# Starting the first expert inside the router stage, turning the weight ring by four slots, and adding the second biases in the last sums

## The reference, cut to what matters

```python
h = layer_norm(DN_ALPHA * h + mixed, ln1_g, ln1_b)
# router: logits, top 4 of 32, softmax over the four
hb = x2[tok] @ w_exp_in[e] + b_exp_in[e]          # 1024 -> 2048
act = min(x_glu, 7) * sigmoid(1.702 * min(x_glu, 7)) * (clip(x_lin, -7, 7) + 1)
y  = (act @ w_exp_out[e] + b_exp_out[e]) * gate    # 1024 -> 1024
h = layer_norm(DN_ALPHA * h + sum over the token's experts of y, ln2_g, ln2_b)
```

## Time and profile before

| what | value |
|---|---|
| median of three runs | 1474.34 us |
| profiled execution, its own time | 1474.43 us |
| its span, first to last instruction | 1472.7 us |
| mean granted TensorE clock | 0.991 |
| PE busy | 1427.1 us, 97% |
| VectorE busy | 1214.7 us, 82% |
| ACT busy | 975.7 us, 66% |
| POOL busy | 490.6 us, 33% |
| barrier between the blocks | 299.3 us |
| PE idle while expert 0 turns into expert 1 | 6.46 us |

### The profile page before, as it was taken

One profiled execution on the slowest core, in us unless ns is written; L12 is line 12 of the kernel. 1 busy time (PEld: TensorE's weight loads), 2 busy tenths in 40 slices (PEclk: granted clock), 3 DMA queues, 4 the chain that ended last, 5 costly groups with the idle time before them and its releaser, 6 DMA issues.

```text
span 1472.7 us, 20375 instructions
## 1 busy us (share of the span) xinstructions
PE 1427.1 (97%) x6495; PEld 1095.9 (74%) x6495; DVE 1214.7 (82%) x1002; ACT 975.7 (66%) x710; POOL 490.6 (33%) x309
## 2 busy tenths in 40 slices
PE   6999989998999999999999999999999999999995
PEld 3466554776888888888888888888888888888873
DVE  5533357577999999999999999999999999999985
ACT  2244660176777777777777777777777777777762
POOL 4200125152333334344333444443343333333101
PEclk9999999999999999999999999999999999999997
DMA  7221226479999999999999999999999999999933
GB/s 260 76 61 36 61 104 261 186 270 360 367 378 379 377 386 385 380 377 371 376 378 384 379 380 390 385 387 382 381 380 378 379 378 381 379 379 378 359 122 126
DMA packets 86310, 461.43 MB, mean 313 GB/s; under 512 B 11912, under 2 KB 26506, under 8 KB 37130
## 3 DMA queue, kind: packets, MB, share of 16 engines
q1 hardware_dynamic: 75190, 431.91, 74.6%
q0 software_dynamic: 9648, 26.49, 7.8%
q10 hardware_dynamic: 1444, 2.66, 0.7%
HBM read 443.92 MB, written 25.76 MB: 319 GB/s over the span
## 4 chain that ended last, share of the span: by engine, by line
PE 75%; DVE 1%; DMA 1%; POOL 1%; issue 1%; POOLq 0%; DVEq 0%; ACT 0%; ACTq 0%
PE banks L1765 69%; PE banks L1733 2%; PE banks L1739 2%; DMA acc_dram<-glu_lin 1%; PE banks L1797 1%; POOL sel L1464 1%; PE banks L1860 0%; POOLq L1466 0%; DVE raw L1694 0%; PE banks L1865 0%; DVEq L1585 0%; DVE raw L1698 0%; PE banks L1727 0%; DVE glu_lin L1581 0%; ACT hi L1352 0%
## 5 line engine op out<-in xcount | busy, mean ns | idle before, releaser
L1544 DVE TENSOR_TENSOR lo<-raw,hi 128x2048 fp32r<-128x2048 f32 x384 | 867.1, 2289 | 75.8 <-ACT hi L1352 75.5
L1352 ACT ACTIVATE hi<-raw 128x2048 fp32r<-128x2048 f32 x384 | 733.7, 1920 | 249.6 <-PE banks L1765 249.4
L1765 PE MATMUL banks<-hi,x_hi 128*128 128x512 f32 x1040 | 286.7, 397 | 8.8 <-DVE x_lo L1568 6.5
L1765 PE MATMUL banks<-lo,x_hi 128*128 128x512 f32 x1040 | 280.1, 391 | 0.0
L1765 PE MATMUL banks<-hi,x_lo 128*128 128x512 f32 x1040 | 278.9, 389 | 0.0
L1464 POOL TENSOR_SCALAR sel<-cst,rank_e 128x128 bf16<-128x128 f32 x120 | 209.7, 1759 | 136.9 <-issue 136.9
L1765 PEld LDWEIGHTS banks<-lo,x_hi 128*128 128x128 f32 x1040 | 195.9, 188 | 41.9
L1765 PEld LDWEIGHTS banks<-hi,x_lo 128*128 128x128 f32 x1040 | 195.4, 188 | 41.4
L1765 PEld LDWEIGHTS banks<-hi,x_hi 128*128 128x128 f32 x1040 | 190.7, 188 | 47.3 <-issue 11.2
L1487 POOL DMA_INDIRECT acc_dram<-ye,dst_row x31 | 50.2, 1620 | 363.5 <-ACT ye L1377 363.5
L1765 PE MATMUL banks<-hi,a_hi 128*128 128x512 f32 x496 | 155.7, 395 | 0.0
(11 more groups left out here) (276 smaller groups left out, 1198.5 us busy)
## 6 DMA issues: line engine op xcount, KB each, us to landing
raw<-in_w_exp_in SPq DMA_DIRECT2D x256, 1024.0 KB, 7.7
raw<-in_w_exp_out SPq DMA_DIRECT2D x128, 1024.0 KB, 7.2
raw<-in_w_in SPq DMA_DIRECT2D x9, 1024.0 KB, 7.6
raw<-in_w_out SPq DMA_DIRECT2D x4, 1024.0 KB, 5.1
x<-in_x SPq DMA_DIRECT2D x4, 512.0 KB, 6.2
h_dram<-x SPq DMA_DIRECT2D x4, 512.0 KB, 3.2
bias_in<-bias_dram SPq DMA_DIRECT2D x128, 3.0 KB
raw<-acc_dram SPq DMA_DIRECT2D x4, 512.0 KB, 5.3
```

Of the source, the lines that this page charges most:

```text
L1352: act.activation(hi[:, c0 % PARTS, :], raw[:, c0 % RAW, :], ACT.Copy).then_inc(hi_done, 1)
L1544: dve.tensor_tensor(lo[:, c0 % PARTS, :], raw[:, c0 % RAW, :], hi[:, c0 % PARTS, :].bitcast(F32), ALU.subtract).then_inc(lo_done, 1)
L1765: last = pe.matmul(psum[:, bank + n, :], s[:, k, :], w[:, at:at + 512], start=(first and m == 0 and new), stop=(closes and m == steps - 1 ...
```

## The change

1. **Ring.** Chunk c0 of the stream now lies in slot (c0 + 4) mod 12, so expert 0's first chunks are among those loaded early. The buffers of block two are laid out in another order, so that new ones fit over the mixer's.
2. **First chunk.** ACT makes `hi0`, the first chunk's hi, ahead of its last copy of `h1T` in block one, VectorE `lo0` before it waits for the logits. ACT makes `hi1`, the second chunk's hi, after the logits; its lo is VectorE's first work of block two.
3. **Expert 0's rows.** The half k below 4 is split in block one (`x0_half_hi`, `x0_half_lo`), the other half in block two; PE waits for the second before chunk 4 only.
4. **Offers.** The two rounds, their copies, their four DMAs and the waits for them are gone, and so are the 18 dummy products. The biases are added in PSUM by `offer(i)` in the last sums: for tiles 0 to 2 ahead of all sums, for tile 3 ahead of its own. `b_exp_out` is loaded near the end of SP's list.
5. **Moved.** The two memsets of `bias_in` go from VectorE to POOL, ahead of POOL's first gather. The overflow count moves to after chunk 6's lo. VectorE's `x_part(1)` stands before `clip(0)`, chunk 10's lo after `swiglu(0)`; ACT's `x_part(1)` comes after chunk 9's hi.

```diff
+                    if i == NT:
+                        act.wait_ge(out_ready, 2 * NT)
+                        act.wait_ge(raw_in[ring_slot(0)], 16)
+                        act.activation(hi0[:, :], raw[:, ring_slot(0), :], ACT.Copy).then_inc(hi_done, 1)
...
+                act.wait_ge(rt_ready, 1)
+                act.wait_ge(raw_in[ring_slot(1)], 16)
+                act.activation(hi1[:, :], raw[:, ring_slot(1), :], ACT.Copy).then_inc(hi_done, 1)
+                act.wait_ge(x0_half_ready, 1)
+                act.activation(x0_hi[:, 0:4, :], psum[:, 6, :]..., ACT.Copy).then_inc(x0_half_hi, 1)
...
+                dve.wait_ge(hi_done, 1)
+                dve.tensor_tensor(lo0[:, :], raw[:, ring_slot(0), :], hi0[:, :].bitcast(F32),
+                                  ALU.subtract).then_inc(lo_done, 1)
                 dve.wait_ge(rt_ready, 1)
...
-                for q in range(1, IN_CHUNKS + AHEAD):
-                    if q - PARTS in OFFER_AT:
-                        offer_part(OFFER_AT.index(q - PARTS))
+                for q in range(3, IN_CHUNKS + AHEAD):
                     part(0, q)
-                act.wait_ge(chunk_used, IN_CHUNKS)
-                x_part(1)
+                    if q == TURN_AT + BEHIND:
+                        x_part(1)
                 gated(0)
...
-                dve.memset(bias_in[0:64, :], 0.0)
-                dve.memset(bias_in[64:P, :], 1.0).then_inc(plus_one_set, 1)
-                x_part(0)
-                for q in range(IN_CHUNKS + AHEAD):
+                part(0, 1)
+                dve.wait_ge(x_hi_done, 1)
+                dve.tensor_tensor(x0_lo[:, 4:KD, :], psum[:, 7, :]..., x0_hi[:, 4:KD, :]...,
+                                  ALU.subtract).then_inc(x_lo_done, 1)
+                for q in range(2, IN_CHUNKS + AHEAD - 1):
                     part(0, q)
+                    if q == TURN_AT:
+                        over_count()
+                x_part(1)
                 clip(0)
-                x_part(1)
                 swiglu(0)
+                part(0, IN_CHUNKS + AHEAD - 1)
...
+                def offer(i):
+                    r = slice(E * i, E * i + E)
+                    for n in range(2):
+                        pe.matmul(psum[:, SUM_BANK[i] + n, :], gateT[r, :], b_out[r, 512 * n:512 * n + 512],
+                                  start=True, stop=False)
...
-                for _ in range(18):
-                    pe.matmul(psum[:, 0, 0:P], ident, ones, start=True, stop=True)
                 first_product(0, 0, 0)
...
+                for i in range(NT):
+                    if SUM_BANK[i] != 4:
+                        offer(i)
                 for i in range(NT):
                     b = SUM_BANK[i]
                     pe.wait_ge(sum_in[i], 16)
                     if b == 4:
                         pe.wait_ge(y_lo_done, 1)
+                        offer(i)
                     for n in range(2):
-                        pe.matmul(psum[:, b + n, :], ident, s[:, i, ...], start=True, stop=False)
+                        pe.matmul(psum[:, b + n, :], ident, s[:, i, ...], start=False, stop=False)
```

More of the change, by code:

```diff
@@ L62 @@
 PICK_AT = 2
-OFFER_AT = (1, 3)
 TURN_AT = 6
@@ L231, in hybrid_layer @@
         ones = cst[:, C_ONES:C_ONES + P]
+        first_parts = ExitStack()
+        hi0 = sb("hi0", [P, CW], F32R, first_parts)
+        lo0 = sb("lo0", [P, CW], F32R, first_parts)
+        x0_hi = sb("x0_hi", [P, KD, SLOTS], F32R, first_parts)
+        x0_lo = sb("x0_lo", [P, KD, SLOTS], F32R, first_parts)
+        hi1 = sb("hi1", [P, CW], F32R, first_parts)
+        first_parts.close()
         mix = ExitStack()
@@ L438, in _ @@
                         sp.wait_ge(out_ready, 2 * NT)
-                        for q in range(MIX_RAW):
-                            ahead(q)
+                        for s in range(MIX_RAW):
+                            ahead(s)
                     sp.wait_ge(h1_ready, i + 1)
@@ L939, in _ @@
                 dve.tensor_copy(dst_row[:, :], slot[:, :, 0])
[L940 to L948, removed]
+                dve.wait_ge(x0_half_hi, 1)
+                dve.tensor_tensor(x0_lo[:, 0:4, :], psum[:, 6, :].rearrange("p (b s) -> p b s", s=SLOTS),
+                                  x0_hi[:, 0:4, :].bitcast(F32), ALU.subtract).then_inc(x0_half_lo, 1)
             @block.tensor
@@ L1172, in _ @@
                                          sel0[:, i, :], start=(i == 0), stop=(i == NT - 1))
+                    if k == 3:
+                        last.then_inc(x0_half_ready, 1)
                 last.then_inc(xT_ready, 1)
@@ L1179, in eb @@
             return sb(name, shape, dt, ex)
+        glu_lin = eb("glu_lin", [P, 2 * F])
+        glu, lin = glu_lin[:, 0:F], glu_lin[:, F:2 * F]
+        ye = eb("ye", [P, D])
+        b_out = eb("b_out", [P, D])
+        a_hi = eb("a_hi", [P, KD, SLOTS], F32R)
+        a_lo = eb("a_lo", [P, KD, SLOTS], F32R)
+        x_hi = eb("x_hi", [P, KD, SLOTS], F32R)
+        x_lo = eb("x_lo", [P, KD, SLOTS], F32R)
         hi = eb("hi", [P, PARTS, CW], F32R)
@@ L1218, in hybrid_layer @@
         y_scaled, scattered = sem("y_scaled"), sem("scattered")
-        over_ready, pool_steps = sem("over_ready"), sem("pool_steps")
-        offer = [glu, lin, ye[:, :], b_out[:, :]]
+        over_known, over_ready, pool_steps = sem("over_known"), sem("over_ready"), sem("pool_steps")
         y_hi = a_hi[:, :, :].rearrange("p k s -> p (k s)")
@@ L1480, in scatter @@
                     pool.wait_ge(y_scaled, v + 1)
[L1481 to L1484, removed]
+                    if not is_first(v):
                         pool.wait_ge(scattered, 16 * v)
@@ L1759, in products @@
                     w_hi, w_lo = hi[:, c0 % PARTS, :], lo[:, c0 % PARTS, :]
+                    if is_first(turn) and c0 == 0:
+                        w_hi, w_lo = hi0[:, :], lo0[:, :]
+                    if is_first(turn) and c0 == 1:
+                        w_hi = hi1[:, :]
                     for m in range(steps):
@@ L1773, in first_product @@
                     x = v + 1 + dummy
-                    pe.wait_ge(x_hi_done, x)
-                    pe.wait_ge(x_lo_done, x)
-                    if not is_first(v):
+                    s_hi, s_lo = (x0_hi, x0_lo) if is_first(v) else (x_hi, x_lo)
+                    if is_first(v):
+                        pe.wait_ge(x0_half_hi, 1)
+                        pe.wait_ge(x0_half_lo, 1)
+                    else:
+                        pe.wait_ge(x_hi_done, x)
+                        pe.wait_ge(x_lo_done, x)
                         pe.wait_ge(lin_ready, v)
@@ L1779, in first_product @@
                     for c in range(IN_CHUNKS):
-                        if is_first(v) and c in OFFER_AT:
-                            offers(OFFER_AT.index(c))
+                        if is_first(v) and c == 4:
+                            pe.wait_ge(x_hi_done, x)
+                            pe.wait_ge(x_lo_done, x)
                         if is_first(v) and c == TURN_AT:
-                            pe.wait_ge(offer_copied, 2 * NT)
                             turn_x(1)
@@ L1790, in first_product @@
                             pick(pick_next)
-                        products(turn, c0 + c, 0, 4, 1, x_hi, x_lo, c, c == 0)
+                        products(turn, c0 + c, 0, 4, 1, s_hi, s_lo, c, c == 0)
                     pe.wait_ge(bias_in_ready, 64 * (v + 1))
@@ L1853, in _ @@
                 pe.wait_ge(gated_ready, E)
+                pe.wait_ge(gateT_copied, 1)
+                pe.wait_ge(b_out_in, 16 * NT)
+                for i in range(NT):
+                    if SUM_BANK[i] != 4:
+                        offer(i)
                 for i in range(NT):
```

113 lines of the change are left out of this document (55 added, 58 removed).

## The result

The changed kernel takes 1458.54 us (median of 4 runs, 1458.27 to 1458.94) against 1474.48 us for the kernel before (4 runs): ratio 0.9891, 95% interval 0.9877 to 0.9904, so 15.9 us less. 1462.7 was forecast with a range down to 1460.3; the direction was right, and the gain was 4 us larger than the sum had it. The profiled execution took 1458.66 us, its span 1456.9 us, 15.8 less than the span before.

The account below looks back on a forecast made before the run. PE was taken to bound the expert loop, so only its idle and non-expert work could change: -5.0 - 2.5 - 5.0 - 1.65 + 2.6 = -11.6 us, giving 1462.7 us, range 1460.3 to 1467.7.

Parts of the forecast that it names:

- The start of block two: PE's first expert product starts at about 299.9 instead of 304.92, since hi0, lo0 and half the rows exist: -5.0 us.
- the offers' rounds: Expert 0's first product loses two rounds of 1.07 us and 0.3 us of restarts: -2.5 us.
- the change of experts: PE's idle between expert 0 and expert 1 falls from 6.46 to 1.4 us: -5.0 us.
- the clock behind it: Expert 1's first eight products no longer run at a clock of 0.5 after the idle: -1.65 us.
- The margins: Slack before PE would wait: lo of early chunks 0.5 us, gathered rows at least 1.8, expert 1's x_lo 1.3.
- 0 was the right value: Cost of lo0 beside POOL's operation in block one, taken as 0, with 0.1 to 0.2 us kept for the range.
- The twelve passes: Bias products of tiles 0 to 2 ahead of the last sums: 2.14 us; tile 3's four passes 1.72 us more.
- The rival that they run mostly in a row: In the last sums the bias products take 4.3 to 5.2 us instead of 2.14: 1464.9 to 1465.8 us; chance 0.24.
- the part on the last sums: End of the kernel: the added bias products delay tile 3's statistics, less POOL contention given back: +2.6 us (2.1 to 5.6).
- the register load stands there: PE's 2.21 us idle ahead of the last sums stays; new products come after it and aren't hidden.
- the slow clock in this stretch: Last sums: tiles 0 and 1 keep 3.90 and 3.09 us instead of 2.65, left unchanged.
- the +2.6 of the new products themselves: Last sums: statistics of tile 3 3.3 us later, 0.7 us back from scaling without POOL beside it.

Follow-up runs that it names:

- The two parts undone: The kernel after with PE waiting for both halves of expert 0's rows, 1463.04 us, and with clip(0) before x_part(1), 1461.35 us.
- b_no_offers: The kernel before without the offers, their copies, accumulating DMAs and waits, the second biases left out: 1467.03 us, ratio 0.9951.
- a_clip_first: The kernel after with VectorE's clip(0) before x_part(1), the old order: 1461.35 us.
- a_inc104: The kernel after with 104 increments of an unused semaphore ahead of PE's first wait: 1467.96 us.
- b_dummies10: The kernel before with 10 of the 18 dummy products, PE's code 32 instructions shorter: 1473.22 us, ratio 0.9993.
- n_dummies26: The kernel before without the offers, with 26 instead of 18 dummy products: 1467.99 us.
- a_inc50: The kernel after with 50 increments of an unused semaphore ahead of PE's first wait: 1459.31 us.
- b_pad152: The kernel before with 152 empty instructions ahead of PE's first wait, which left no record in the trace, taken as a repeat: 1474.31 us.
- a_no_offer: The kernel after without the offers in the last sums, the second biases left out: 1456.54 us.
- a_whole_rows: The kernel after with PE waiting for both halves of expert 0's rows before chunk 0: 1463.04 us.

## Why the prediction was wrong, point by point

**The start of block two, the offers' rounds, the change of experts, the clock behind it.** Right, each to 0.2 us. The two parts undone confirm that PE's start and x_part's place are on the path. The margins held: PE didn't wait for lo, for the gathered rows (issued at 303.85) or for a bias. x_lo of expert 1 ended 0.47 us before clip could start (322.45 against 322.92), a smaller margin than the 1.3 I gave it, and the idle became 1.49, not 1.4. Of the 5.0 us at the change of experts, 2.8 were the DMA's (`b_no_offers`), 1.0 the order of clip and x_part (`a_clip_first`), and about 1.2 the lo of chunk 10, which the sum didn't price by itself.

The first chunk's lo0 and POOL's operation ran side by side for 1.3 us, and both had their usual lengths, 2.29 and 2.77 us. So 0 was the right value. The lock-out that the Trainium skill (SBUF — State Buffer, SBUF: two separate sides) states didn't show in this pair.

**The twelve passes.** Right: 1.94 us against 2.14, and 1.91 against 1.72 for tile 3. The rival that they run mostly in a row is ruled out; twelve in three groups and sixteen in four took the same time, and in the trace the twelve start in four sets of three, 0.43 us from set to set. By the strict order of starts that the Trainium skill (TensorE: Matmul & The Clock Gate, The mechanism) states, I had estimated 4.3 us; the measurement decides.

**The step that failed** is in the part on the last sums: "the register load stands there. The new products come after this load, so they aren't hidden in it", and with it the slow clock in this stretch, of which it says "I leave as it is". Both the idle and the clock were kept at their old size, as if they belonged to the place in the program. The register load was 0.5 us in PE's queue in both kernels, and in the kernel before it began at 1438.7, over 4 us ahead of the last product's end. The 2.21 us were the tail of the branch behind it, 5.4 us, and the branch was slow by the position of PE's code; the change took some 104 instructions away ahead of it. That gave back 2.21 us of idle and, as in `a_inc104` in reverse, the clock: 3.90 + 3.09 - 2.75 - 2.65 = 1.59 us. Together 3.8 us against a miss of 3.7 in this stage; the +2.6 of the new products themselves held. The other way round, 104 increments in the new kernel brought idle and slow clock back. That both the branch and the clock were fast again is luck as far as the edit goes, since nothing in it was meant to do this.

What stands behind the branch's two durations is shown as far as this. It follows the length of the code ahead of it, in three sets of kernels: before and `b_dummies10`, `b_no_offers` and `n_dummies26`, after with `a_inc104` and `a_inc50`. The accumulator's four loads were issued about a microsecond ahead of fast branches too (from 1424.08 in the kernel after, from 1438.81 in `b_dummies10`), so they don't decide it. And in all four slow executions a transfer of instructions, 16 KB, falls into the branch, for the kernel before in the window from 1439.7 to 1444.9 us (transfers, MB, share of the engines):

```profile
q8 instruction: 1, 0.02, 1.1%
```

The times of that transfer and of the branch, in us of each trace:

| run | branch starts | transfer | branch ends | PE's next product |
|---|---|---|---|---|
| before | 1439.60 | 1442.65 to 1443.58 | 1445.00 | 1445.16 |
| `b_pad152` | 1439.57 | 1444.31 to 1445.26 | 1446.68 | 1446.85 |
| `n_dummies26` | 1434.32 | 1437.54 to 1438.47 | 1439.90 | 1440.06 |
| `a_inc104` | 1429.84 | 1433.57 to 1434.51 | 1435.94 | 1436.21 |

Each time the branch ends 1.4 us after the transfer does, however late that comes. That speaks for a branch that waits for the transfer, but it is inferred from these four: nothing was run that moves the transfer alone. That a transfer lies there would say little by itself, since the fast kernels have one too, 2.9 to 4.7 us after the branch's start, when theirs has long ended.

The Trainium skill (Runtime: NRT & Kernel Launch, Instruction fetch mechanics) says that code is fetched in blocks of 16 KB, 256 instructions, ahead in a straight line, and that a taken branch to a block outside the window waits for the fetch. The trace agrees in the size of the transfer, in the branch's end behind it, and in that 32 instructions of code more or less turn it; that the transfer holds the branch's target is not shown. With that in view, a fast branch would have been a rival at about 1459 (1462.7 less the 3.8 us above), with its sign in the branch's own row. The transfer began 3.1 to 4.7 us after the branch did; what it waited for isn't settled.

**A second size.** Against the kernel before, whose slow branch had hidden the wait for the selection matrix, the new products cost the 2.6 us forecast. Against a kernel with a fast branch they cost 2.0 us (`a_no_offer`), since PE would otherwise wait 1.14 us for that matrix.

## What to carry to other kernels

An idle time that the trace puts to "issue" can have an owner all the same: look at the engine's queue rows just before it, the branches and register loads, before deciding what stays. If it is a slow branch, an edit that changes the amount of code ahead of it can remove or create it, here 1.2 to 4.8 us of the last sums; so an edit worth a few microseconds is to be compared by the stages it touches, with the branch's duration beside them. Removing dummy products can let the clock fall when they filled a wait, as in `b_dummies10`, where only a DMA's wait further on hid the cost.

## What the runs showed of the hardware that I had not expected

- The same branch took 0.36 to 0.47 us or 5.4 to 7.1 us, and 32 instructions of difference in the code before it turn it. When it was slow, it ended 1.4 us after a transfer of instructions.
- Behind a single idle of PE the granted clock fell to 0.5 after 2.21 us (before, last sums), 2.51 (`a_clip_first`), 2.81 (`b_dummies10`) and once after 1.64 (`a_inc104`). It stayed at 1.0 after 1.49 (after), 2.39 (`n_dummies26`) and 2.95 (`a_whole_rows`). So the length of the idle alone doesn't tell.
- Two products for each of three row groups take 1.94 us and for each of four 1.95 us.
- The time between a span's end and the execution's end isn't fixed: 1.7 us in most, 2.1, 2.4 and 3.2 us in `a_inc50`, `b_dummies10` and `b_no_offers`. These three also have an instruction transfer in their last microseconds, but `n_dummies26` has 2.3 us without one, so the transfer doesn't explain all of it.
